# Six half slabs of weight remainders go from GpSimd to VectorE in the attention units of a two-layer streaming encoder

## What is computed

```python
z = x @ w_in                       # [q_A | k_A | v_A | c_q | c_kv | k_rope]
y_a = window_attention(...)        # mixer A: 8 heads, sinks, relative bias
q = rms(c_q) @ w_uq; q_lat = q_nope @ w_uk
scores = (q_lat @ ckv.T + q_rope @ krope.T) * MLA_SCALE
o_lat = softmax(scores) @ ckv      # mixer B: the streams also attend to 512 cached rows
y_b = o_lat @ w_uv
g = sigmoid(x @ w_gate + b_gate)   # 2048 columns
h = g[:, :D] * (y_a @ w_proj_a) + g[:, D:] * (y_b @ w_proj_b)
x = LN1(ALPHA * x + h @ w_out)
x = LN2(ALPHA * x + ConvGLU(x))    # up 1024 -> 2 * 2816, conv, gelu, down
```

## Time and profile before

| | us |
|---|---|
| median of 3 runs | 1887.1 (1885.34 to 1888.52) |
| the profiled execution | 1887.02 |
| its span, first to last instruction | 1885.2 |
| PE busy | 1843.2 |
| DVE busy | 1010.5 |
| ACT busy | 655.1 |
| POOL busy | 540.6 |
| mean granted clock of TensorE | 0.994 of full speed |

### The profile page before, as it was taken

One profiled execution on the slowest core, in us unless ns is written; L12 is line 12 of the kernel. 1 busy time (PEld: TensorE's weight loads), 2 busy tenths in 40 slices (PEclk: granted clock), 3 DMA queues, 4 the chain that ended last, 5 costly groups with the idle time before them and its releaser, 6 DMA issues. The chain is left out here.

```text
span 1885.2 us, 31852 instructions
## 1 busy us (share of the span) xinstructions
PE 1843.2 (98%) x12458; PEld 1752.6 (93%) x12458; DVE 1010.5 (54%) x1597; ACT 655.1 (35%) x1381; POOL 540.6 (29%) x244
## 2 busy tenths in 40 slices
PE   8999999999999999999999999999999999999996
PEld 8987887999999999999999888889999999999995
DVE  3576544359754333444776765444696443244447
ACT  4245443333433212332322644333334331133323
POOL 2331211134143244333422322112323333443331
PEclk9999999999999999999999999999999999999998
DMA  7262322321121122211242623214211211222121
GB/s 227 100 163 70 127 84 89 125 107 68 68 90 61 67 73 90 89 50 56 89 137 71 157 76 121 92 64 145 102 68 68 89 56 67 82 85 89 42 75 57
DMA packets 67003, 171.20 MB, mean 91 GB/s; under 512 B 16376, under 2 KB 33456, under 8 KB 59056
## 3 DMA queue, kind: packets, MB, share of 16 engines
q1 hardware_dynamic: 66896, 169.72, 27.4%
HBM read 152.47 MB, written 19.61 MB: 91 GB/s over the span
## 5 line engine op out<-in xcount | busy, mean ns | idle before, releaser
L719 POOL TENSOR_TENSOR w_lo<-w_raw,w_hi 128x1024 fp32r<-128x1024 f32 (+2 forms) x230 | 530.3, 2314 | 1270.6 <-ACT w_hi L806 1251.4
L806 ACT ACTIVATE w_hi<-w_raw 128x1024 fp32r<-128x1024 f32 (+2 forms) x228 | 218.3, 975 | 438.1 <-PE ps L1668 431.8
L1668 PE MATMUL ps<-x_hi,w_hi 128*128 128x320 f32 x1408 | 321.6, 309 | 0.0
L1668 PE MATMUL ps<-x_hi,w_lo 128*128 128x320 f32 x1408 | 320.7, 309 | 0.0
L1668 PE MATMUL ps<-x_lo,w_hi 128*128 128x320 f32 x1408 | 320.7, 309 | 0.0
L1668 PEld LDWEIGHTS ps<-x_hi,w_hi 128*128 128x128 f32 x1408 | 235.4, 188 | 0.3
L1668 PEld LDWEIGHTS ps<-x_lo,w_hi 128*128 128x128 f32 x1408 | 235.5, 188 | 0.0
L1668 PEld LDWEIGHTS ps<-x_hi,w_lo 128*128 128x128 f32 x1408 | 235.3, 188 | 0.0
L1568 DVE TENSOR_SCALAR f_conv<-f_ext,vec 128x656 f32<-128x656 f32 x44 | 63.9, 1452 | 202.9 <-ACT tail L1036 200.5
L1935 PE MATMUL ps<-x_hi,w_hi 128*128 128x320 f32 x512 | 163.6, 319 | 1.5 <-ACT logits L896 1.5
L1935 PE MATMUL ps<-x_hi,w_lo 128*128 128x320 f32 x512 | 158.3, 309 | 0.0
(11 more groups left out here) (298 smaller groups left out, 3191.2 us busy)
## 6 DMA issues: line engine op xcount, KB each, us to landing
w_raw<-in_slabs SPq DMA_DIRECT2D x84, 1024.0 KB, 4.9
w_raw<-in_slabs SPq DMA_DIRECT2D x20, 768.0 KB, 4.0
gate_logits<-logits SPq DMA_DIRECT2D x64, 160.0 KB, 1.9
gates<-gate_logits SPq DMA_DIRECT2D x16, 640.0 KB, 6.4
w_raw<-in_slabs SPq DMA_DIRECT2D x16, 640.0 KB, 3.8
ckvc<-in_ckvc SPq DMA_DIRECT2D x16, 256.0 KB, 2.7
ckvc_t<-in_ckvc_t SPq DMA_DIRECT2D x16, 256.0 KB, 3.0
w_raw<-in_slabs SPq DMA_DIRECT2D x6, 512.0 KB, 5.9
```

The source lines that it names most:

```text
L719: pool.tensor_tensor(to, w_raw[:, s % 2, c], hi.bitcast(F32), ALU.subtract).then_inc(wlo_ready, 1)
L806: A(w_hi[:, s % 2, c], w_raw[:, s % 2, c], ACT.Copy).then_inc(whi_ready, 1)
L1668: ins = MM(out_[:, a, :], w, x[:, t, a * HT:(a + 1) * HT], start=t == 0 and w is wh and x is hi, stop=t == tiles - 1 and w is wl)
```

## The change

For six slabs of each layer, 12 to 17 (the last four gate slabs and the first two projection slabs), VectorE makes the low part of the second half, and GpSimd only that of the first. VectorE does it in its step u, behind `take_out(u - 1)`, for a second half that ScalarE cast behind unit u - 1. By the order of the gates, that falls in VectorE's steps 13, 18, 23, 29, 34 and 39, for slabs 12, 13, 14, 15, 16 and 17. GpSimd waits for VectorE's count before it passes the half on and frees the raw buffer. The counts at the layer norms are raised to match.

```diff
--- before.py
+++ after.py
@@ -113,10 +113,18 @@
 
 
 
+SHARED = [S_GATE + 4 + k for k in range(6)]
+
+
 
 def low_count(layer, which):
 
-    return 3 + 3 * (2 * layer + which + 1) if layer >= 0 else 3
+    return 3 + 3 * (2 * layer + which + 1) + len(SHARED) * (layer + 1) if layer >= 0 else 3
+
+
+def shared_count(layer, s):
+
+    return 3 + (6 + len(SHARED)) * layer + SHARED.index(s) + 1
 
 
 def half_slab(s, half):
@@ -742,6 +750,8 @@
                 for s in range(3, S_UP1 + 1):
                     if s == S_UQ + 1:
                         low_rotary(s)
+                    elif s in SHARED:
+                        low(s, s, layer, shared_count(layer, s))
                     else:
                         low(s, s, layer)
                 low(S_UP1 + 1, S_UP1 + 1, layer, low_count(layer, 0) - 2)
@@ -1340,10 +1350,16 @@
                         dve.wait_ge(kv_stored, (layer + 1) * 32)
                     if u >= 1:
                         take_out(u - 1)
+                        for g in gate_behind(u - 1):
+                            t = S_GATE + 2 + g // 4
+                            if g % 4 == 3 and t in SHARED:
+                                weights_low(w_lo[:, t % 2, :], w_hi[:, t % 2, :], t, 1, layer * (2 * NS) + 2 * t + 2)
                     if u - 1 in YA_HIGH:
                         ya_low(YA_HIGH.index(u - 1))
                 take_out(NU - 1)
                 ya_low(3)
+                for g in gate_behind(NU - 1):
+                    assert g % 4 != 3
 
                 job(J_UV)
                 dve.tensor_copy(y_b[:, :, SEQ:], ps[:, 2 * (J_UV % 4), :].rearrange("p (k n) -> p k n", k=4)
```

## The result

| | kernel before | kernel after |
|---|---|---|
| median | 1887.43 us | 1898.46 us |
| from, to (6 runs each) | 1885.34 to 1889.12 | 1897.80 to 1899.95 |
| ratio | | 1.0060 [1.0048, 1.0072] |
| profiled execution, span | 1887.02, 1885.2 us | 1898.38, 1896.6 us |
| mean granted clock | 0.994 | 0.990 |

The ratio, with its 95% interval, is taken from all the runs of both kernels; it is not the quotient of the medians. The change makes the kernel slower by 11.0 us of the medians, or 11.4 us between the two profiled executions. 7.3 us and at most 1897.0 had been forecast: the direction and the chain of causes came out, the time lies above the range.

A forecast was written before the change was run, and what follows sets the result against it. PE was taken to bound the kernel, busy 1843.2 of 1885.2 us. From 1887.0: +6.4 (two waits), +2.7 (clock), -0.7 and -1.1 (waits that go) = +7.3, thus 1894.3 us; range 1889.5 to 1897.0.

The forecast's parts named there:

- PE waits for the caches: Before the first stream's scores, PE waits 3.0 us in layer 0 and 3.4 in layer 1, 6.4 together.
- clock behind the two waits: A clock drop behind each wait for the caches, 2 x 1.4 = 2.7 us.
- the wait of 0.34 goes, twice: PE's wait at 207.88 goes in both layers as VectorE catches up while PE waits: -0.7 us.
- the wait of 0.56 goes, twice: PE's wait before the transposes at 248.50 goes with GpSimd's half of slab 14, in both layers: -1.1 us.
- The freeing and the queue: Slab 12's buffer is freed later, so SyncE issues slab 14, with the caches behind it, 3.56 us later, at 200.81.
- The passing-on: From the end of VectorE's subtraction to slab 14's issue: 0.40 us taken, 0.14 kept as the other end.
- The landing: `krc_t` lands 5.9 us (layer 0) or 6.3 us (layer 1) behind its issue, as before.
- The rule of the Trainium skill: Fixed 2.0 us plus 436 GB/s: slab and caches land at about 206.6, PE waits 1.5 us per layer, sum about +1.
- the place at 350 us: PE stood still 2.5 us, then the clock was 0.50 for 2.8 us; that drop cost 1.4 us.
- Rival (a): The wait for the caches comes but the clock holds: +4.6, 1891.6 us; chance 0.22.
- The start of the kernel: PE waited 3.8 us there and the clock at 10 to 15 us was 1.00, evidence against a drop.
- VectorE's added work: Twelve subtractions of 1.22 us, 14.7 us on a half-idle engine, costed at nothing for PE.

The follow-up runs named there:

- Run 1: Changed kernel with the first stream's caches queued ahead of slab 14 in SyncE's queue instead of behind it: 1884.22 us, ratio 0.9989.
- run 2: Kernel before, with SyncE's load of slab 14 held until VectorE has normalised unit 15, GpSimd making all low halves: 1900.94 us, ratio 1.0075.
- Run 9: Changed kernel with the gate job run ahead of scores and transposes, behind PE's wait for the first stream's caches: 1894.40 us, ratio 1.0040.
- run 5: Kernel before, with SyncE's load of slab 14 held until VectorE has taken out unit 12: 1895.43 us, ratio 1.0051.
- run 6: Kernel before, with SyncE's load of slab 14 held until VectorE has taken out unit 13: 1908.29 us, ratio 1.0114.
- run 7: Changed kernel with four useless matmuls ahead of the first stream's scores in each layer: 1891.22 us, ratio 1.0022.
- run 3: Changed kernel with only slab 12's second half on VectorE, the other five staying on GpSimd: 1900.97 us, ratio 1.0077.
- Run 4: Changed kernel with the second halves of slabs 13 to 17 on VectorE, slab 12's staying on GpSimd: 1883.69 us, ratio 0.9985.
- run 10: Changed kernel with only the second half of slab 14 (gate 19) on VectorE: 1884.74 us, ratio 0.9985.
- run 8: Kernel before, GpSimd making all halves, with the first stream's caches queued ahead of slab 14: 1885.40 us, ratio 0.9999.

## Why the prediction was right, and where it failed

Between the profiled executions, per term of its sum (us):

| term | predicted | measured | from |
|---|---|---|---|
| PE waits for the caches | +6.4 | +7.2 | 3.67 + 3.57 |
| clock behind the two waits | +2.7 | +8.1 | 4.4 + 3.7 |
| the wait of 0.34 goes, twice | -0.7 | -0.7 | not there in either layer |
| the wait of 0.56 goes, twice | -1.1 | -1.1 | not there in either layer |
| everything else | 0 | -2.1 | below |
| sum | +7.3 | +11.4 | |

**The freeing and the queue: right.** The twelve subtractions run at 1.22 us, slab 14 goes out at 200.60 (200.81 predicted), PE stops before the scores and for a transfer. The passing-on took 0.22 us instead of 0.40, nearer the other end; that made the wait smaller by 0.2. The landing took 6.7 and 6.6 us instead of the 5.9 and 6.3 kept from before; that and 0.1 us from the landing to the start of the scores made it longer. Runs 1 and 2 show the step from both sides: the order taken away, the loss goes; the late issue alone, the loss comes.

The rule of the Trainium skill that the prediction weighed ("DMA: Bandwidth & Descriptors", Anatomy of one DMA) would have had slab and caches landed 5.8 us after the slab's issue, at 206.4; they landed at 208.7, 8.1 us after it. The trace decides against the rule once more.

**The clock: right in kind, wrong in size, and this is the step that failed.** The prediction took "2 x 1.4" from the place at 350 us (its like in layer 1, at 1281 us, has a drop as well). It took a stop of 3.0 to 3.4 us for the same kind of case as the one of 2.5, and did not ask what PE does behind it. Run 9 shows that as the difference: with gate matmuls first the low stretch is 3.3 us, near the 2.8 that the prediction used, with scores first 9.7. Runs 5 and 6 show that the length of the wait is not what sets the price between 2.2 and 7.2 us. (Behind the 1.91 us of run 5's layer 1 the low stretch was short as well, 3.4 us, although scores came first; the clock fell late there, when most of the scores were done. The kind of work is therefore not all of it.) The term was 8.1 us by the rows and 7.2 by run 7. With it in place of 2.7 the sum would have been 1899 to 1900, and a range as wide around that would have held the time. Rival (a), the clock holds, is refuted by all twelve waits for the caches at which PE stood still in after and in runs 2, 3, 5, 6 and 9: the clock fell at each. The start of the kernel, which spoke for it, was misread. The 1.00 at 10 to 15 us in the earlier trace rows is no measurement: the trace's record of the clock begins at 14.3 us, and a window without a record reads 1.00. The pace tells it. PE of before, behind the wait of 3.8 us and after 14.3 us:

```profile
8.22 0.61 PE L1689 MATMUL ps<-x_hi,w_hi 128*128 128x320 f32 x1 [3.79 <-ACT x_hi L777]
...
11.55 0.47 PE L1689 MATMUL ps<-x_hi,w_hi 128*128 128x320 f32 x1
...
15.67 0.31 PE L1689 MATMUL ps<-x_hi,w_lo 128*128 128x320 f32 x1
```

Up to about 14 us the matmuls of 320 columns take 0.47 us and start 0.27 us apart, as after's gate matmuls do at a granted 0.50; behind it they take 0.31 and start 0.15 apart, as at 1.00. So PE ran at half speed for some 6 us there, with dense matmuls. The earlier trace rows had the hint: 22 matmuls in 5.00 us, against 32 in 4.60. Read by its pace, the start would have spoken against (a), and for a price above 1.4 us.

**VectorE's added work: right, costs nothing.** Run 1 has all of it and is faster than before. Run 4 too, with ten of the twelve. The prediction counted 14.7 us more for VectorE; the page has 3.0 (1013.5 against 1010.5). Operations that GpSimd's subtraction used to hold up take their usual time now, as the row under the next heading shows for one.

**The waits that go: right.** GpSimd's subtraction beside slab 12 is gone from 194.70, and VectorE's small operation at 194.87 takes 0.16 us where the same one took 2.22 in before:

```profile
194.90 2.22 DVE L1272 SCALAR_TENSOR_TENSOR st_nm<-st_mx,nsink_s 128x1 f32<-128x1 f32 x1
```

The Trainium skill says of this ("SBUF — State Buffer", Who interferes with whom) that an operation of VectorE that uses the port pair shared with GpSimd blocks for the whole of GpSimd's instruction; the trace agrees for this operation of 128x1 elements, which ended at 197.12, as GpSimd's subtraction did at 197.11. The wait at 207.88 is gone because VectorE caught up while PE stood, and it is back in runs 1, 4 and 10, as it should be.

**What the -2.1 us are.** PE's lead or lag can be followed along equal instructions. Late in the attention of layer 0 (a wait for `y_b`) after is behind by 350.85 - 343.81 = 7.04 us; early in that of layer 1 by 1122.64 - 1117.27 = 5.37. PE of before, three such instructions:

```profile
343.81 0.91 PE L1916 MATMUL ps<-probs_t,ckvc 128*128 128x128 f32 x6 [0.48 <-DVE y_b L1318]
...
1117.27 0.44 PE L1869 MATMUL ps<-ident,probs 128*128 128x128 f32 x2 [0.46 <-DVE probs L1294]
...
1271.99 0.68 PE L1916 MATMUL ps<-probs_t,ckvc 128*128 128x128 f32 x4 [0.49 <-DVE y_b L1318]
```

PE of after, the same three, and the wait ahead of the next stage:

```profile
350.85 0.91 PE L1932 MATMUL ps<-probs_t,ckvc 128*128 128x128 f32 x6 [0.49 <-DVE y_b L1328]
...
359.65 0.54 PE L1684 MATMUL ps<-yb_hi,w_hi 128*128 128x320 f32 x2 [2.51 <-DVE yb_lo L1369]
...
1122.64 0.44 PE L1885 MATMUL ps<-ident,probs 128*128 128x128 f32 x2 [0.46 <-DVE probs L1304]
...
1283.59 0.68 PE L1932 MATMUL ps<-probs_t,ckvc 128*128 128x128 f32 x4 [0.48 <-DVE y_b L1328]
```

Of the 1.7 us won back, 1.4 are the drop at 350 us itself: after has the same wait of 2.51 us there, but the clock behind it stayed up this time, as the window shows:

```profile
359.60:362.40 2.80, 2.75 (x19) 2.78 (x20) 2.11 (x3) 2.77 (x4) 0.00 (x0) 1.00 0.67 254
```

At this place the clock fell in 16 of 24 cases (two layers in each of the twelve profiled kernels), with the same wait and the same work. Why in some and not in others was not found out. I count it as scatter and not as the change's doing, which is not shown, since each kernel was profiled once. The remaining 0.7 of the 2.1 us are small differences that I did not follow up. In layer 1 the lag grows by 1283.59 - 1271.99 - 5.37 = 6.2 us: 3.57 of wait, 3.7 of clock, less the 0.9 of the two waits that go. Layer 1 repeats layer 0, as was assumed.

**What stays open** is the exact size of the gain: 1.1 us by the waits that go, 2 to 3 us by the medians of runs 4 and 10, whose intervals reach from 1.1 to 4.5 us below before. Part of it may be the drops at 350 us and at its like in layer 1: in the profiled executions before had two of them, run 8 one, run 1 none, run 4 one, run 10 two. At equal number the gain is 2.1 us (1887.02 against 1884.88, run 10) and 1.6 us (run 8 at 1885.40 against run 4 at 1883.76), one execution each.

**A version that beats both.** Runs 1, 4 and 10 are faster than before and than after: 1884.22, 1883.69 and 1884.74 us, 0.11% to 0.15% below before, at the edge of what can be told.

## What to carry to other kernels

Before the freeing of a buffer is moved to another engine, read the queue that refills it: everything behind that load, small and urgent loads first, inherits the delay; here a slab loaded 3.35 us later stopped TensorE once in each layer. A stop of TensorE is to be priced with the clock behind it, from a place in the trace with the same kind of work behind the stop; here the clock cost as much as the stop (8.1 beside 7.2 us). Where a stop could not be avoided, matmuls of no use in it gave back nearly all of the clock's part here (7.2 us), dense ones behind it about half (4.1 us). Before a granted clock of 1.00 is taken from a window, the pace of equal matmuls should be looked at as well.

## What the runs showed of the hardware

- The granted clock fell to 0.50 at each of twelve waits for a transfer of 1.9 to 7.2 us, in most of them before the wait was over. At the wait of 1.91 us it fell only 2.3 us after work had begun again.
- Counted from the start of work, the stretch at 0.50 lasted 7.8 to 9.8 us with scores and transposes first (8.6 behind the longest wait, 9.8 behind one of 2.20 us), but 3.4 us behind the wait of 1.91 us, where it began late, and 3.3 to 3.4 us with gate matmuls first. At the kernel's start, with dense matmuls, it was some 6 us by their pace. By scores to values a drop cost 3.5 us (run 3, 9.73 and 9.72 us against 6.2) to 4.5 us (run 5, layer 0), and 1.45 where it came late; 0.43 to 0.46 us for each microsecond of work at 0.50.
- With four useless matmuls of 512 columns in the wait it did not fall.
- Behind one and the same wait of 2.51 us it fell in 16 of 24 cases.
